# Strassen's scheme for the input projections of the second part of a two-part transformer kernel

## The reference, cut to what matters

```
h   = rms_norm(x, mix_pre_gain)         # (512, 1024)
qkv = h @ w_in                          # (512, 1024) @ (1024, 3072)
q, k, v = split(qkv, 3)                 # each (512, 1024)
q, k = rotary(q), rotary(k)             # 16 of each 64 columns are rotated
... attention, output projection, norm, residual
```

## Time and profile before

| | us |
|---|---|
| median of 3 runs | 3157.65 (3156.69 to 3160.12) |
| the profiled execution | 3155.12 |
| its span, first to last instruction | 3153.3 |
| granted TensorE clock, mean | 0.981 |
| PE busy | 2946.8 (93%) |
| DVE, ACT, POOL busy | 914.0, 649.6, 436.6 |

### The profile page before, as it was taken

The page is one execution under the profiler, slowest core; times in us unless marked ns, Lnnn a source line. Parts: engine busy times, 40 slices in busy tenths (PEclk is TensorE's granted clock), DMA queues, the critical chain, the costliest instruction groups (busy, mean ns, idle before and its releaser), DMA issues.

```text
span 3153.3 us, 29756 instructions
## 1 busy us (share of the span) xinstructions
PE 2946.8 (93%) x11556; PEld 1714.0 (54%) x11556; DVE 914.0 (29%) x2018; ACT 649.6 (21%) x1448; POOL 436.6 (14%) x693
## 2 busy tenths in 40 slices
PE   7999988889999987899999999999998899999999
PEld 4465533244655432344655588854444564688844
DVE  3533311145343111203622234300215722333301
ACT  3332210123322100102622211100104522211100
POOL 2001111121011110101310011200002610022200
PEclk9999999899999999999999999999999999999999
DMA  3114599931135999521021122222211021122121
GB/s 144 47 47 166 209 419 412 392 127 47 47 130 220 398 415 407 185 80 54 1 81 54 54 81 80 90 84 80 75 62 51 1 83 51 68 93 81 67 107 53
DMA packets 112103, 421.19 MB, mean 134 GB/s; under 512 B 9169, under 2 KB 13393, under 8 KB 84177
## 3 DMA queue, kind: packets, MB, share of 16 engines
q1 hardware_dynamic: 98736, 383.62, 31.7%
q0 software_dynamic: 12640, 33.45, 2.8%
q10 hardware_dynamic: 576, 2.10, 0.2%
HBM read 408.64 MB, written 27.26 MB: 138 GB/s over the span
## 4 chain that ended last, share of the span: by engine, by line
PE 77%; DMA 9%; issue 7%; DVE 4%; ACT 2%; DVEq 1%; SPq 0%; POOL 0%; POOLq 0%; ACTq 0%
PE ps L2627 15%; PE ps L402 13%; PE ps L2296 11%; PE ps L2397 6%; DMA ring_feat<-in_w 5%; PE ps L2777 5%; PE ps L1587 4%; PE ps L1067 4%; PE ps L2417 3%; DMA big<-in_w 2%; PE ps L1627 2%; PE ps L2691 2%; PE ps L1850 1%; PE ps L1862 1%; PE ps L2488 1%
## 5 line engine op out<-in xcount | busy, mean ns | idle before, releaser
L2296 PE MATMUL ps<-ring_feat 128*128 128x512 f32 x768 | 333.0, 596 | 2.1 <-DVE ring_feat L337 2.1
L402 PE MATMUL ps<-ring_feat 128*96 128x512 f32 (+3 forms) x768 | 307.4, 556 | 14.5 <-DMA ring_feat<-in_w_lat 5.5
L2777 PE MATMUL ps<-ring_feat,tmp 128*128 128x512 f32 x704 | 302.8, 592 | 0.0
L2296 PEld LDWEIGHTS ps<-ring_feat 128*128 128x128 f32 x768 | 146.5, 191 | 185.4 <-issue 184.7
L402 PEld LDWEIGHTS ps<-ring_feat 128*128 128x128 f32 (+1 forms) x768 | 140.1, 185 | 166.6 <-issue 122.1
L2777 PEld LDWEIGHTS ps<-ring_feat,tmp 128*128 128x128 f32 x704 | 133.6, 190 | 166.5 <-issue 166.4
L2627 PE MATMUL ps<-big 128*128 128x256 f32 x960 | 213.7, 379 | 0.0
L2397 PE MATMUL ps<-ring_feat 128*128 128x512 f32 x448 | 194.6, 593 | 2.9 <-ACT ring_feat L2543 2.2
L2627 PEld LDWEIGHTS ps<-big 128*128 128x128 f32 x960 | 182.4, 190 | 24.8
L2353 DVE TENSOR_TENSOR big<-ps,par 128x512 f32<-128x512 f32 x48 | 33.1, 691 | 468.5 <-ACT big L2349 468.5
L1587 PE MATMUL ps<-big,tmp 128*64 128x512 f32 x512 | 123.6, 632 | 33.0 <-DMA big<-in_w 30.1
(11 more groups left out here) (413 smaller groups left out, 3968.5 us busy)
## 6 DMA issues: line engine op xcount, KB each, us to landing
big<-in_w SPq DMA_DIRECT2D x48, 2048.0 KB, 16.9
ring_feat<-in_w SPq DMA_DIRECT2D x48, 2048.0 KB, 15.0
ring_feat<-in_w_gate_up SPq DMA_DIRECT2D x22, 2048.0 KB, 8.0
ring_feat<-in_w_mix_in SPq DMA_DIRECT2D x12, 2048.0 KB, 8.4
ring_feat<-in_w_down SPq DMA_DIRECT2D x10, 2048.0 KB, 7.3
tmp<-in_w_mem_kv SPq DMA_DIRECT2D x6, 2048.0 KB, 20.6
ring_feat<-in_w_out SPq DMA_DIRECT2D x4, 2048.0 KB, 9.1
big<-expert_out SPq DMA_DIRECT2D x16, 512.0 KB, 8.5
```

Of the source, the lines that this page charges most:

```text
L402: yield T.matmul(bank, lhs(k), rhs(k), start=k == 0, stop=k == n - 1)
L2296: yield T.matmul(bank, featv[:, k, t * P:(t + 1) * P], w[:, k, :], start=k == 0, stop=k == KC - 1)
L2777: return T.matmul(banks[t, half], hidden[:, k, t * P:(t + 1) * P], w[:, j, half * 512:(half + 1) * 512], start=k == 0, stop=k == FC - 1)
```

## The change

Column block 0 is computed as before. Column blocks 1 to 5 are each computed in two groups `g`. A group takes token tiles `g` and `g + 2` and the two halves (256 columns each) of the weight block; the blocks of the scheme are input chunks 0 to 3 and 4 to 7, the two token tiles, and the two column halves. The stationary operand is 128x128 of the features or of their sums, the moving one 256 columns of the weights or of their differences.

- Sums of the features are formed once a layer by VectorE (`sums(featv)`, into the head of `tmp`), in block 0 after the last tile is turned.
- Differences of each weight block are formed by VectorE into **one** buffer, `mix_w_diff` (`tmp`, 4096 on). For block 1 this stands in block 0, right behind the sums of the features; for block c+1 it stands in block c ahead of group 1's reads, behind a wait for group 1's last product that uses the differences.
- Products are ordered so that those that need no differences stand at the end of group 1 (8 matmuls) and at the start of group 0 (8 and 4 matmuls).
- ScalarE copies 3 half banks a group, VectorE makes 4 additions, GpSimd 3, where before 4 copies of 128x512 stood for a block.
- Attention on TensorE also waits for the last group's additions on GpSimd and VectorE (`mix_settled`).
- The rotation's work space moves to `tmp`, 10240 on. It comes after the additions of each group of block 4, two tiles at a time.
- The semaphore counts are now by stage ("mix", "gate"), layer and group; `feature_differences` becomes `differences` and the inner part of `weight_sums` becomes `sums`. `gate_up` and `down_projection` keep their instructions.

```diff
+        mix_feat_sum = [view(tmp, i * 1024, KC // 2, 256) for i in range(4)]
+        mix_w_diff = [view(tmp, 4096 + i * 1024, KC // 2, 256) for i in range(4)]
+        mix_staged = [view(tmp, 8192 + i * 256, 256) for i in range(8)]
...
+        def differences(dve, w, sums):
+            lo, hi = w[:, LOW_K, :], w[:, HIGH_K, :]
+            t1, t2, t3, t4 = sums
+            V.tensor_tensor(t1, lo[:, :, HI], lo[:, :, LO], ALU.subtract)
+            V.tensor_tensor(t3, hi[:, :, HI], lo[:, :, HI], ALU.subtract)
+            dve.drain()
+            V.tensor_tensor(t2, hi[:, :, HI], t1, ALU.subtract)
+            dve.drain()
+            V.tensor_tensor(t4, hi[:, :, LO], t2, ALU.subtract).then_inc(blocks_summed, 1)
...
+        def mix_group(name, eng, l, c, g, w, block_end):
+            n = 2 * (c - 1) + g
+            p1_, p7_, p5_, u2 = mix_staged[4 * g:4 * g + 4]
+            first, second = split_banks(mix_banks[l][g])
+            lo_t, hi_t = [slice((g + d) * P, (g + d + 1) * P) for d in (0, 2)]
...
+            if name == "pe":
+                if c > 1:
+                    eng.wait_ge(hidden_ready, g_dve("mix", l, n - 2, MIX_C21))
+                def plain():
+                    block_product(first[0], featv[:, LOW_K, lo_t], w[:, LOW_K, LO])
+                    return block_product(second[0], featv[:, HIGH_K, lo_t], w[:, HIGH_K, LO])
+                if g == 0:
+                    plain().then_inc(up_full, 1)
+                    if c == 1:
+                        eng.wait_ge(blocks_summed, g_sums("mix", l, 0))
+                    block_product(second[3], s4, w[:, HIGH_K, HI])
+                    eng.wait_ge(blocks_summed, g_sums("mix", l, c))
+                block_product(first[1], s2, t2).then_inc(up_full, 1)
+                block_product(first[2], s3, t3)
+                block_product(second[2], s1, t1).then_inc(up_full, 1)
+                m = block_product(first[3], featv[:, HIGH_K, hi_t], t4)
+                if g:
+                    m = block_product(second[3], s4, w[:, HIGH_K, HI])
+                m.then_inc(up_full, 1)
+                if g:
+                    plain().then_inc(bank_full, 1)
...
+            if name == "dve":
+                eng.wait_ge(silu_ready, g_act("mix", l, n, read["P1"]))
+                V.tensor_tensor(out[:, g, LO], p1_, second[0], ALU.add).then_inc(hidden_ready, 1)
+                eng.wait_ge(up_full, g_full("mix", l, n, full["P6"]))
+                V.tensor_tensor(u2, p1_, first[1], ALU.add).then_inc(hidden_ready, 1)
+                eng.wait_ge(up_full, g_full("mix", l, n, full["P4_P3"]))
+                eng.wait_ge(outer_added, g_pool("mix", l, n, MIX_U4))
+                V.tensor_tensor(out[:, g, HI], p5_, second[3], ALU.add).then_inc(hidden_ready, 1)
+                V.tensor_tensor(out[:, g + 2, LO], p7_, first[3], ALU.add).then_inc(hidden_ready, 1)
+            if name == "pool":
+                eng.wait_ge(hidden_ready, g_dve("mix", l, n, MIX_U2))
+                eng.wait_ge(silu_ready, g_act("mix", l, n, read["P5"]))
+                G.tensor_tensor(out=p7_, in0=p7_, in1=u2, op=ALU.add).then_inc(outer_added, 1)
+                eng.drain()
+                G.tensor_tensor(out=out[:, g + 2, HI], in0=p7_, in1=p5_, op=ALU.add).then_inc(outer_added, 1)
+                eng.drain()
+                G.tensor_tensor(out=p5_, in0=p5_, in1=u2, op=ALU.add).then_inc(outer_added, 1)
...
         def mix_projection(name, eng, l):
...
+                        if t == (1 if l == 0 else 0):
+                            turn_x(name, eng, TT - 1)
+                            if name == "dve":
+                                eng.drain()
+                                sums(eng, featv, mix_feat_sum)
+                                mix_weights(eng, l, n + 1, 1)
...
+                        if name == "dve" and g and c < 5:
+                            eng.wait_ge(up_full, g_full("mix", l, 2 * (c - 1) + 1, MIX_FULL[1]["P4_P3"]))
+                            mix_weights(eng, l, n + 1, c + 1)
+                        mix_group(name, eng, l, c, g, w, block_end)
+                        if name == "dve" and c == 4:
+                            if g == 0:
+                                eng.wait_ge(bank_read_act, copied)
+                                eng.wait_ge(outer_added, g_pool("mix", l, 2 * 2 + 1, MIX_C22))
+                                eng.drain()
+                            for t in (2 * g, 2 * g + 1):
+                                rotate_tile(eng, t)
```

More of the change, by code:

```diff
@@ L1806, in rotate_tile @@
             c, s = (r[:, t, :].unsqueeze(1).to_broadcast([P, n, half]) for r in (cos2, sin2))
-            work = [view(tmp, k * n * half, n, half) for k in range(4)]
+            work = [view(tmp, 10 * D + k * n * half, n, half) for k in range(4)]
             rotate(dve, hh[:, :, 0:half], hh[:, :, half:ROT], c, s, work, half)
@@ new lines, in block_product, with split_banks @@
+        def block_product(to, lhs, rhs):
+            for j in range(KC // 2):
+                m = T.matmul(to, lhs[:, j, :], rhs[:, j, :], start=j == 0, stop=j == KC // 2 - 1)
+            return m
+        def split_banks(four):
+            return [[ps[:, q, h * 256:(h + 1) * 256] for q in four] for h in range(2)]
+        MIX_FULL = [dict(P1_P2=0, P6=1, P7_P5=2, P4_P3=3), dict(P6=0, P7_P5=1, P4_P3=2)]
+        MIX_READ = [dict(P1=0, P7=1, P5=2), dict(P7=0, P5=1, P1=2)]
+        MIX_C11, MIX_U2, MIX_C12, MIX_C21 = range(4)
@@ L2288, in mix_projection @@
                     eng.wait_ge(w_loaded[n % 2], 16 * (n // 2 + 1))
-                for t in range(TT):
-                    if name == "pe":
[L2291 to L2311, removed]
@@ L2572, in program @@
         U3_READY, HIGH_UP, U4_READY = range(3)
[L2573 to L2610, removed]
         def fast_chunk(name, eng, l, k, w, block_end, after_u2=None):
             b, i = divmod(k, 2)
-            n = l * FAST + k - 2
+            n = k - 2
             cols = slice(i * P, (i + 1) * P)
             p1_, p7_, p5_, u2, low, high = quarters[6 * (n % 2):6 * (n % 2) + 6]
-            first, second = [[ps[:, q, h * 256:(h + 1) * 256] for q in fast_banks[l][n % 2]] for h in range(2)]
+            first, second = split_banks(fast_banks[l][n % 2])
             if name == "pe":
@@ L2622, in fast_chunk @@
                 t1, t2, t3, t4 = feat_diff
[L2623 to L2628, removed]
-                if k >= 4:
[L2631 to L2639, removed]
+                lo, hi = LOW_K, HIGH_K
+                if k >= 4:
+                    eng.wait_ge(hidden_ready, g_dve("gate", l, n - 2, LOW_UP))
+                block_product(first[0], gate[:, lo, :], featv[:, lo, LO])
+                block_product(second[0], gate[:, hi, :], featv[:, hi, LO]).then_inc(up_full, 1)
+                eng.wait_ge(blocks_summed, g_sums("gate", l, b))
+                block_product(first[1], s2, t2).then_inc(up_full, 1)
+                block_product(first[2], s3, t3)
+                block_product(second[2], s1, t1).then_inc(up_full, 1)
+                block_product(first[3], up[:, hi, :], t4)
+                block_product(second[3], s4, featv[:, hi, HI]).then_inc(bank_full if i else up_full, 1)
             if name == "act":
```

133 lines of the change are left out of this document (109 added, 24 removed).

## The result

| us | before | changed |
|---|---|---|
| median | 3157.17 (3156.61 to 3160.12, 4 runs) | 3135.71 (3133.52 to 3138.01, 4 runs) |
| profiled execution | 3155.12 | 3134.92 |
| its span | 3153.3 | 3133.1 |

The ratio is 0.993, 95% interval 0.9913 to 0.9947: 21.5 us faster (0.7%), at 3135.71 us where 3136.4 was forecast.

The account below looks back on a forecast made before the run. TensorE's issue rate times the number of products bounds the touched stage. 3155.12 - 33.0 (products) + 8.4 (pauses) + 3.4 (clock) = 3133.9 us profiled; the median stands 2.5 above, so 3136.4, range 3130 to 3146.

Parts of the forecast that it names:

- Saved products: Blocks 1 to 5: 137.4 us of matmuls replaced by ten groups of 12.09 us, saving 16.5 us a layer, 33.0 in both.
- Rival 3: Block products: half-width products 5 to 10% slower here, 12 to 24 us, giving 3154 us, no measurable change; chance 0.05.
- Differences with one buffer: VectorE's weight differences between blocks: 4.97 us covered by 20 TensorE matmuls with 3.4 us of slack, costed at nothing.
- Rival 4: Block boundaries: the single buffer serialises, TensorE waits at 8 boundaries, up to 3194 us when fully exposed; chance 0.04.
- Block 4's rotation: VectorE in block 4: two rotated tiles, 2.34 us each, done at 19.5 us, before the differences' start at 20.7.
- Rival 2: Small waits in block 4 or at layer 0's entry, 1 to 2 us at each of 4 places, 3142 us; chance 0.13.
- The start of a layer: Feature sums and block 1's differences, 5.0 + 5.0 us, ready at about 1326 us in layer 0, costing nothing.
- The pause: TensorE between the last product and attention: 4.9 us instead of 0.69, +4.2 us a layer, +8.4 in both.
- The clock: Attention's opening: half rate for the first 2 to 6 us, +1.7 us a layer, +3.4 in both.
- rival 1: Attention's opening: the clock stays at full rate despite the 4.9 us without matmuls, giving 3133.0 us; chance 0.20.
- sum for the profiled execution: Whole kernel: 3155.12 - 33.0 + 8.4 + 3.4 = 3133.9 us for the profiled execution.
- tail of 4.9 us: End of each layer's stage: ScalarE, VectorE and GpSimd finish the last group's additions, uncovered, before attention; 4.9 us.

Follow-up runs that it names:

- two loaded runs: Changed kernel plus two or five extra 128x1024 VectorE operations ahead of each weight block's differences (blocks 2 to 5): 3134.0 and 3165.1 us.
- reordered run: Changed kernel with only the product order of each layer's very last group changed, the 8 matmuls without differences first: 3125.29 us, ratio 0.9898.
- filled pause: Changed kernel plus 10 TensorE matmuls into an unread bank between the last product and attention: 3133.27 us, ratio 0.9927.
- run with five more operations: Changed kernel plus five VectorE operations of 128x1024 ahead of each weight block's differences (blocks 2 to 5), +6.4 us each time: 3165.1 us, ratio 1.0023.
- fillers: Changed kernel plus 10 or 4 TensorE matmuls into an unread bank before attention: 3133.27 and 3133.68 us.

## Why the prediction was right

- **Saved products.** 16.5 us a layer was forecast; 16.46 and 16.47 came. The duration of a group from the gate and up products carried over to other operands and buffers unchanged (12.09). Rival 3, slower half-width products, is out.
- **Differences with one buffer.** Costed at nothing because of 3.4 us of slack behind 20 matmuls. The changed kernel shows no wait. The two loaded runs confine the slack to between 2.6 and 6.4 us, and the 2.9 us left of the latter put it at 3.5. Rival 4 was a real mechanism with the price foreseen per boundary: with VectorE 6.4 us late it made the kernel slower than before.
- **Block 4's rotation.** Forecast to end at 19.5 us and be needed at 20.7; VectorE's 1.52 us of idle time is that margin. Rival 2 did not occur.
- **The start of a layer.** The differences were ready at 1326.6 us in layer 0, as forecast but for the shift of a microsecond. Block 1 begins at 1328.9 with products that need no differences; its first product that reads them starts at 1334.07, so that the margin was 7.5 us.
- **The pause.** +4.2 forecast, +4.07 measured. The reordered run shows that it was avoidable: 0.94.
- **The clock.** The fall was forecast from the earlier trace rows and came in both layers; the filled pause proves cause and size in layer 1. The forecast time alone could not have told it from rival 1 (3133.0, which is 2.7 us from the median): the windows at 0.50 and 0.52 do. That 1.7 us a layer met 1.66 and 1.87 so closely is partly luck, since two errors cancelled. Half rate lasted longer than the 2 to 6 us expected: 9.3 us of attention's opening in layer 0 and 6.6 in layer 1. And work at half rate did not add its own length, as the prediction had it. TensorE was busy for 7.76 and 5.13 us there, half of which, 3.9 and 2.6, is what half rate added; only 1.66 and 1.87 reached the end of attention. In layer 0 the wait for GpSimd ahead of L1850, 2.10 us before and 0.44 after, took up 1.66 of it. The Trainium skill, "TensorE: Matmul & The Clock Gate", section "HAM oscillation — how this bites in real kernels", expects the price once per such wait. The changed kernel agrees, with two waits and two falls; the run with five more operations agrees only in part, with five falls behind eight waits of 2.9 to 3.3 us.
- **The remainder.** The sum for the profiled execution was -21.2, measured -20.2; 1.05 us of the difference arose ahead of the touched stage, in code that is the same. There the ten profiles lie between 1313.67 and 1318.23 us, so this is scatter; that the median came within 0.7 us of the forecast is luck to that extent.

What the prediction did not say, though its own numbers held it, is that the tail of 4.9 us had a cheap remedy: the order of the last group gave 4.8 us in layer 0 and 5.8 in layer 1.

## What to carry to other kernels

When an algorithm trades matmuls for additions on other engines, and TensorE never waits in the stage, the saving is TensorE's time for a matmul times the matmuls saved. Here it could be read from a stage that already ran in the new form. Then look at the two ends: what the slowest chain of additions leaves uncovered after the last product, and which products of the last group could be issued before those that the chain does not need. A buffer need not be doubled if the products that don't read it are put together around its rewriting; count that cover in matmuls against the rewriting and its signals, and remember that beyond it a wait is paid in itself and, behind five of the eight waits here, a second time in the clock.

## What was not expected of the hardware

The length of a pause alone did not decide whether the clock fell. With five more operations, waits of 2.92 us in the same code were followed by half rate in five cases and left the rate whole in two, as did one of 3.27 us. Pauses of 3.04 us lost it twice. A pause of 0.94 us ahead of attention kept it in layer 1 of the run with the last group reordered and lost it in layer 0, and in both layers of the run with every group 1 reordered; each time the fall came some 3 us into the opening. Attention's opening, with no wait over 2.1 us, kept the clock in the kernel before, but lost it in layer 0 with the pause filled.

The same happens where nothing was changed. From the memory queries' first product of the table above to the first gate product, each profile takes either 183.8 or 185.5 us in either layer. It is 185.5 in exactly those layers in which a spell of half rate lies in this stretch, as in the kernel before in layer 0 (mean granted clock 0.73 from 1735.8 to 1742.2 us) and not in layer 1. The short falls outside the changed pause come and go between kernels whose code there is the same, cost 0.7 to 1.7 us each, and are part of the scatter that hid the small gains of the fillers. What decides them stays open.
